# A two-layer decoder with a routed mixture of experts: gates applied before the rows are stored, and accumulating DMAs in place of VectorE sums

## The reference, cut to what matters

```python
D_MODEL = 1024; BATCH = 1; SEQ = 512; DEPTH = 2
N_EXPERTS = 16      # 4 groups of 4; top-1 group, then top-2 experts in it
EXPERT_FF = 512

h = x
for i in range(DEPTH):
    hn = rms_norm(h, norm_mix[i])
    h = h + (short_conv_mixer(...) if i == 0 else dilated_attention_mixer(...))
    hn = rms_norm(h, norm_ffn[i])
    h = h + hierarchical_moe(hn, ...)
return rms_norm(h, norm_final)

# hierarchical_moe: combine[t, e] is the gate of token t for expert e, nonzero for its two experts
out = 0
for e in range(N_EXPERTS):
    a = silu(t @ w_gate[e]) * (t @ w_up[e])
    out = out + combine[:, e:e + 1] * (a @ w_down[e])
```

## Time and profile before

| what | value |
|---|---|
| device time, median of 3 runs | 1442.1 us (1441.58 to 1443.96) |
| the profiled execution's own time | 1443.29 us |
| its span, first to last instruction | 1441.6 us |
| PE busy | 1352.6 us, 94% of the span |
| DVE busy | 992.9 us, 69% |
| ACT busy | 784.2 us, 54% |
| POOL busy | 209.7 us, 15% |
| moved by DMA | 308.40 MB, 214 GB/s on average |
| mean TensorE clock granted | 0.977 |

### The profile page before, as it was taken

How to read it: one execution, slowest core, us unless ns; L and a number is a source line. 1 busy time by engine, 2 the same in 40 slices (tenths; PEclk the granted TensorE clock), 3 DMA queues, 4 the chain that set the end, 5 groups by cost and what they waited for, 6 DMA issues and landing times.

```text
span 1441.6 us, 20619 instructions
## 1 busy us (share of the span) xinstructions
PE 1352.6 (94%) x7119; PEld 1114.9 (77%) x7119; DVE 992.9 (69%) x1300; ACT 784.2 (54%) x949; POOL 209.7 (15%) x309
## 2 busy tenths in 40 slices
PE   5999986999999999999998999999988799999995
PEld 4888775888888877888877788887767588888884
DVE  6354367999899896252558545344866799989998
ACT  4222244788888853533356253324734388888883
POOL 4000021111111302020200111120002111111131
PEclk9999996999999999999999999999999799999998
DMA  6228515999999964232210222231015699999994
GB/s 222 88 88 306 203 53 210 362 389 389 390 390 392 377 254 163 64 112 88 88 59 2 88 88 88 88 114 62 2 45 216 231 378 390 392 380 390 388 353 174
DMA packets 85105, 308.40 MB, mean 214 GB/s; under 512 B 12033, under 2 KB 12057, under 8 KB 68660
## 3 DMA queue, kind: packets, MB, share of 16 engines
q1 hardware_dynamic: 76404, 291.73, 54.5%
q0 software_dynamic: 8640, 15.86, 2.9%
HBM read 291.72 MB, written 31.46 MB: 224 GB/s over the span
## 4 chain that ended last, share of the span: by engine, by line
PE 86%; DVE 7%; issue 2%; ACT 2%; DMA 1%; SPq 1%; POOLq 0%; DVEq 0%; POOL 0%; ACTq 0%
PE ps L321 26%; PE ps L323 25%; PE ps L322 25%; PE ps L1812 2%; PE ps L1607 1%; PE ps L1885 1%; PE ps L1798 1%; DVE probT L1399 1%; DMA x_rows<-hn_rows,tok_list 1%; DVE h L1215 1%; ACT prob L851 1%; ACT W_hi L727 1%; PE ps L1783 1%; PE ps L1622 1%; PE ps L1512 1%
## 5 line engine op out<-in xcount | busy, mean ns | idle before, releaser
L321 PE MATMUL ps<-W_hi,xT_hi_all 128*128 128x512 f32 x1408 | 558.7, 397 | 3.2 <-DVE rope_b L1467 1.5
L323 PE MATMUL ps<-W_hi,xT_lo_all 128*128 128x512 f32 x1408 | 551.1, 391 | 0.0
L322 PE MATMUL ps<-W_lo,xT_hi_all 128*128 128x512 f32 x1408 | 549.6, 390 | 0.0
L1144 DVE TENSOR_TENSOR W_lo<-m_raw,W_hi 128x2048 fp32r<-128x2048 f32 x192 | 435.8, 2291 | 59.0 <-ACT W_hi L727 58.6
L727 ACT ACTIVATE W_hi<-m_raw 128x2048 fp32r<-128x2048 f32 x192 | 367.2, 1914 | 47.7 <-PE ps L323 47.1
L321 PEld LDWEIGHTS ps<-W_hi,xT_hi_all 128*128 128x128 f32 x1408 | 265.0, 188 | 63.6 <-issue 7.1
L323 PEld LDWEIGHTS ps<-W_hi,xT_lo_all 128*128 128x128 f32 x1408 | 264.9, 188 | 57.3
L322 PEld LDWEIGHTS ps<-W_lo,xT_hi_all 128*128 128x128 f32 x1408 | 265.3, 188 | 52.0
L949 DVE SCALAR_TENSOR_TENSOR W_lo<-raw,mix_gain,W_hi 128x512 fp32r<-128x512 f32 x144 | 99.7, 754 | 178.3 <-ACT W_hi L671 178.3
L671 ACT ACTIVATE W_hi<-raw,mix_gain 128x512 fp32r<-128x512 f32 x144 | 92.2, 712 | 220.2 <-issue 211.4
L637 POOL TENSOR_TENSOR qk_rot<-rope_a,rope_b 128x512 f32<-128x512 f32 x48 | 62.3, 1303 | 370.7 <-DVE rope_b L1467 370.7
(11 more groups left out here) (242 smaller groups left out, 1440.4 us busy)
## 6 DMA issues: line engine op xcount, KB each, us to landing
m_raw<-in_w_gate_dram SPq DMA_DIRECT2D x64, 1024.0 KB, 7.5
m_raw<-in_w_up_dram SPq DMA_DIRECT2D x64, 1024.0 KB, 8.9
m_raw<-in_w_down_dram SPq DMA_DIRECT2D x64, 1024.0 KB, 7.5
raw<-in_attn_w_qkv_dram SPq DMA_DIRECT2D x36, 1024.0 KB, 5.0
raw<-in_conv_w_in_dram SPq DMA_DIRECT2D x12, 1024.0 KB, 5.2
y_rows<-zero_rows SPq DMA_DIRECT2D x2, 4096.0 KB, 17.5
y_pick<-y_rows SPq DMA_DIRECT2D x16, 512.0 KB, 7.0
raw<-in_conv_w_out_dram SPq DMA_DIRECT2D x4, 1024.0 KB, 5.9
```

The lines of the kernel that those rows point to most:

```text
L321: pe.matmul(o, a_hi, b_hi, start=first, stop=False)
L322: pe.matmul(o, a_hi, b_lo, start=False, stop=False)
L323: return pe.matmul(o, a_lo, b_hi, start=False, stop=last)
L1144: dve.tensor_tensor(MW_lo[c % MSPLIT][:, :, :], m_raw[c % MRAW][:, :, :], MW_hi[c % MSPLIT][:, :, :].bitcast(F), ALU.subtract).then_inc(s[ ...
```

## The change

Three parts go together.

1. **Gates.** `y_out` on ACT multiplies each expert row by its gate while it copies the row out of PSUM, with a column `gate_col` of 128 gates as scale. POOL fills that column for each item (`gate_of`), inside `store`, between the copy of the destinations and the scatter; that of item 0 comes after `gather(1)`. ACT waits for it with a new semaphore `gate_col`.
2. **Sums.** `y_back` on SP is gone, and the eight `y_pick` buffers with it. POOL issues, after its last scatter has landed, eight DMAs of 512 KB that read `y_dram[l]` and add to `h[:, r, :]` in SBUF (`accum_op=ALU.add`): first pick 0 of the four row tiles, then pick 1 of each, once its pick 0 has landed.
3. **DVE.** The 16 `stored_rows` are gone. `last_rows` waits for both DMAs of its row tile (`pick_in` at 32) as well as for `placed`.

```diff
@@ last_rows, first_rows, last_layer_rows on DVE
-            def stored_rows(l, r, c):
-
-                dve.wait_ge(M[l]["pick_in"][r], 32)
-                return dve.scalar_tensor_tensor(out=h[:, r, :], in0=y_pick[2 * r + c][:, :],
-                                                scalar=gates[:, c, r:r + 1], in1=h[:, r, :], op0=ALU.mult, op1=ALU.add)
-
             def last_rows(l, r):
                 dve.wait_ge(M[l]["placed"], r + 1)
+                dve.wait_ge(M[l]["pick_in"][r], 32)
                 dve.tensor_tensor(h[:, r, :], ps[:, 2 * r:2 * r + 2, :].rearrange("p a n -> p (a n)"), h[:, r, :],
                                   ALU.add).then_inc(h_ready, 1)
...
@@ moe_rows on POOL
+                def gate_of(i):
+                    pool.tensor_copy(gate_col[:, :], gate_list[:, bass.ds(block_of(i), 1)]).then_inc(s["gate_col"], 1)
+
-                def store(i):
+                def store(i, next_gate=True):
                     pool.wait_ge(s["y"], i + 2)
                     pool.tensor_copy(dest_col[:, :], dest_list[:, bass.ds(block_of(i), 1)]).then_inc(s["dest"], 1)
                     pool.wait_ge(s["dest"], i + 1)
                     pool.sem_inc(pool_passed, 1)
+                    if next_gate:
+                        gate_of(i + 1)
                     pool.indirect_dma_start(y_dram[l], ...)
...
                 gather(1)
+                pool.wait_ge(s["gate_copied"], 1)
+                gate_of(0)
                 pool.wait_ge(s["turned"], 2)
...
-                store(third_last_item(pool))
+                store(third_last_item(pool), next_gate=False)
+                pool.wait_ge(s["ystored"], before_last * 16)
+                pool.sem_inc(pool_passed, 1)
+                for c in range(2):
+                    for r in range(NT):
+                        if c:
+                            pool.wait_ge(s["pick_in"][r], 16)
+                        pool.dma_start(h[:, r, :], y_dram[l][c * S + r * P:c * S + (r + 1) * P, :], accum_op=ALU.add
+                                       ).then_inc(s["pick_in"][r], 16)
@@ y_out on ACT
-                def y_out(unit, stored):
+                def y_out(i, unit, stored):
                     act.wait_ge(s["done"], unit + MSPLIT + 1)
+                    act.wait_ge(s["gate_col"], i + 1)
                     if stored is not None:
                         act.wait_ge(s["ystored"], stored)
-                    act.activation(y_rows[:, :], ps[:, 5:7, :].rearrange("p a n -> p (a n)"), ACT.Copy
-                                   ).then_inc(s["y"], 1)
+                    act.activation(y_rows[:, :], ps[:, 5:7, :].rearrange("p a n -> p (a n)"), ACT.Copy,
+                                   scale=gate_col[:, :]).then_inc(s["y"], 1)
@@ SP
-            def y_back(l):
...
             qkv_unit(0, 0, 0)
-            y_back(0)
             for j in range(1, 3):
                 qkv_unit(j, 0, 0)
...
-            y_back(1)
```

More of the change, by code:

```diff
@@ L112, in build @@
         y_rows = at("y_rows_sb", [P, D], F, E + int(52.25 * KB))
-        y_pick = [at(f"y_pick{i}", [P, D], F, E + int((4 * i if i < 6 else 56.25 + 4 * (i - 6)) * KB))
-                  for i in range(2 * NT)]
         qkT = at("qkT", [P, NATT, 2, 4, S], F, E)
@@ L167, in build @@
         exp_of_half, cand_j, cand_c = (small[:, n:n + 1] for n in range(3))
-        last_gate, last_tok = small[:, 3:5], small[:, 5:7]
+        last_gate, last_tok, gate_col = small[:, 3:5], small[:, 5:7], small[:, 7:8]
         cos_t = keep("cos_t", [P, NT, HD])
@@ L312, in build @@
                 "alo", "y", "ystored", "col", "dest", "gate_ready", "gate_listed", "gate_copied", "last_cols",
-                "last_ready", "last_hi", "last_lo", "placed")})
+                "last_ready", "last_hi", "last_lo", "placed", "gate_col")})
             M[l]["raw_in"] = [sem(f"m{l}_raw_in{i}") for i in range(MRAW)]
@@ L407, in later_weights @@
                 down(l, expert(later), 4, later)
-            def y_back(l):
-                later = later_items(sp)
-                sp.wait_ge(M[l]["ystored"], before_last_item(sp) * 16)
-                sp.sem_inc(sp_passed, 1)
-                for r in range(NT):
-                    sp.wait_ge(M[l]["lo"], later * 6 + (MRAW + 1 + r))
-                    sp.sem_inc(sp_passed, 1)
-                    for c in range(2):
-                        sp.dma_start(y_pick[2 * r + c][:, :], y_dram[l][c * S + r * P:c * S + (r + 1) * P, :]
-                                     ).then_inc(M[l]["pick_in"][r], 16)
             def qkv_unit(j, rev, chunk):
@@ L782, in step @@
                     if y_before:
-                        y_out(i * 6 + 3, stored)
+                        y_out(i - 1, i * 6 + 3, stored)
                     act_hi(i)
@@ L797, in experts @@
                 m_hi(l, 6, before_last)
-                y_out(before_last * 6 + 3, third_last * 16)
+                y_out(third_last, before_last * 6 + 3, third_last * 16)
                 act_hi(before_last)
@@ L1224, in first_rows @@
             def first_rows():
-                after(stored_rows(0, 0, 0))
-                after(stored_rows(0, 0, 1))
-                after(stored_rows(0, 1, 0))
                 last_split(0, 1, slice(3, 5))
-                after(stored_rows(0, 1, 1))
                 last_rows(0, 0)
@@ L1235, in first_rows @@
                 lo(U_QKV + 1)
-                after(stored_rows(0, 2, 0))
                 turn_lo(2, 1)
-                after(stored_rows(0, 2, 1))
                 last_rows(0, 2)
-                after(stored_rows(0, 3, 0))
-                after(stored_rows(0, 3, 1))
                 last_rows(0, 3)
```

15 lines of the change are left out of this document (3 added, 12 removed).

## The result

The changed kernel took **1448.18 us** (median of 5 runs, 1445.48 to 1449.77) where the kernel before took 1442.85 us (1441.58 to 1443.96) beside it: ratio 1.0035, 95% interval 1.0024 to 1.0046, so slower by 5.3 us. The prediction was 1436.9 us, faster. The profiled execution of the changed kernel took 1449.77 us, with a span of 1448.0 us (before: 1443.29 and 1441.6).

The account below looks back on a forecast made before the run. The prediction took TensorE, 94% busy, as the bound, VectorE's sums counting only where TensorE waits or has finished. 5.0 us at the end and 0.2 in layer 0 gave −5.2: 1438.1 profiled, 1436.9 us as median; range 1435.8 to 1452.

Parts of the forecast that it names:

- 5.0 us less at the end: Last layer: without VectorE's eight sums, the last norm starts at 1431.4 in place of 1436.42, 5.0 us less.
- Nothing in the loop: Expert loop: the scaled `y_out` and the gate copy ahead of the scatter cost nothing, with 2.3 us of cover.
- the rival on the loop: Expert loop: scatter lands over 14.1 us after `y_out`, or 0.11 us unhidden; 3 us or more given back; chance 0.03.
- u = 2.0: Both layers' ends: time one adding DMA (0.524 MB) takes the DMA engines with eight queued, taken as 2.0 us.
- 5u − 10.15: Layer 0: loss in us, if positive, from waiting for the fifth adding DMA, wanted at 523.3; zero at 2.0.
- 8u − 19.7: Last layer: loss in us, if positive, from waiting for the eighth adding DMA, wanted at 1428.0; zero at 2.0.
- start + 3.8 + 5u: Layer 0: landing time of the fifth adding DMA, pick 1 of tile 0, with the start at 509.7.
- The accumulate becomes the bound: `last_rows`, both layers: adding DMAs at 4.0 us make TensorE wait 9.9 and VectorE 12.3 us, 1459 us; chance 0.20.
- POOL makes the descriptors slowly: Adding DMAs on POOL: each would take 3.15 us by POOL, as two gathers did, giving 1448 us; chance 0.09.

Follow-up runs that it names:

- e3_last_copies: The changed kernel with layer 0's picks by plain reads and VectorE sums, and the last layer's eight DMAs as plain copies without adding: 1439.81 us.
- e6_two_tiles: The changed kernel with plain reads and VectorE sums in layer 0 and for the last layer's tiles 0 and 1; four adding DMAs remain: 1441.12 us.
- e10_two_held: e6_two_tiles with the four adding DMAs held until the four plain reads of tiles 0 and 1 have landed: 1439.83 us, ratio to before 0.9976.
- e1_hold_qkv: The changed kernel with layer 0's second and third qkv weight loads held on SP until both picks of tile 0 were added: 1453.11 us.

## Why the prediction was wrong, point by point

- **5.0 us less at the end: right in size, not reached.** e3_last_copies (4.86), e6_two_tiles and e10_two_held (4.8) give it. The change gave 3.2, because the picks of tiles 0 and 1 were not in `h` by then, and a norm waited 0.62 us on an `hn` buffer. The prediction had dated only the eighth DMA for the last layer, with a start of 1404.5 that stood 14.1 us ahead of the split; the start was 12.35 ahead, and the fifth and sixth held `last_rows` 0 and 1. It had ruled the buffer out with a landing time of 2.6 us, measured with no adding DMA on the way; here that store took 4.2 us (1435.31 to 1439.53).
- **Nothing in the loop: right.** The bounds on `y_out` (1.12, measured 1.10) and on gate copy with scatter (2.7 us more at most) held, and the thirteen items from the first to the last `y_out` took 227.4 us for 227.7. A slip in the rival on the loop did no harm: its 14.1 us count from the issue of the scatter, not from `y_out`, from where the cover is 17.5.
- **u = 2.0: mis-sized, it is 2.5** (2.48 from the window, 2.47 to 2.64 from the landings). The argument "a plain DMA already reads and writes at once, so the write has no price of its own; the second read comes from SBUF" gave the second operand half a price; the 211 GB/s against 374 in the same queue say that adding makes the DMA 1.77 times as long. That it is the reading of `h` that costs this, no run shows. The Trainium skill (Collectives: The Full Stack, the section on the bandwidth ceiling) has a reducing DMA at about half the rate of a copy. The measured ratio is 0.56, so as a ratio the rule was nearer than my 2.0 and than the 259 GB/s that I had scaled from the absolute figure in the Trainium skill.
- **That alone would not have lost.** By the prediction's own lines, u = 2.5 costs 5u − 10.15 = 2.35 us in layer 0 and 8u − 19.7 = 0.3 at the end, 1439.6 us in all. **The step that failed is the date of the fifth DMA in layer 0**, start + 3.8 + 5u. The start was right (509.7 forecast; 511.14 on a clock that ran 1.5 late). But the 1.05 MB loads that SP now issued ahead were charged to the last scatter ("2 MB now move beside the last scatter of layer 0") and not to the picks behind it: the first adding DMA took 8.4 us to land, not 6.3. e1_hold_qkv took them away and got 5.9. The two together, 2.35 and 2.1, make 4.4 us, and TensorE's transposes came 4.3 us late. (The 0.35 us of slack behind `last_rows` are 0.38 by the rows, 524.93 − 524.55, which changes nothing.)
- **The prediction gave the stall no price beyond its length.** TensorE waited 4.1 us; then its clock was about 0.50 until 536, and the stage from the transposes of tile 0 (530.72) to the last turned tile (551.76) took 21.0 us for 18.8, 2.3 us more. So the stage's 6.5 us are 4.3 up to the transposes and 2.3 behind them. That the clock, and not something else, made the 2.3 is read from the lengths of the same products (0.63 for 0.40 us), and from the 5 us in which they ran at half the clock, which are worth some 2.4. e1_hold_qkv repeated it behind a longer stall. No run separated clock from stall.
- **The rivals.** "The accumulate becomes the bound" named the right place, VectorE's `last_rows` in layer 0, and gave it 0.20; but it put the point from which the kernel is slower at u = 2.92, and with the loads ahead and the clock it lies below 2.5. "POOL makes the descriptors slowly" is refuted by e3_last_copies and by issues of 0.84 to 0.93 us. The range, up to 1452, held the time; the direction, to which 0.54 had gone, was wrong.
- **Left open.** The first 1.5 us of the changed kernel's profile, ahead of the last split of layer 0, are within what such profiles differ by; they stand ahead of the first `y_out` (272.11 for 270.02). The 1.2 us at the very end, behind the last norm, come again in all four kernels in which GpSimd issues sixteen such DMAs; why, I did not take apart. And adding DMAs in the first order with the loads neither ahead of them nor held up until 525 were not tried.
